# First mixer: the low part of every second weight half, from the differential queries' second half to the differential values', is made by GpSimd instead of VectorE

## What is computed

```python
xn = _rms_norm(x, attn_norm[l])
h = xn @ w_in[l]
(h_cq, h_ckv, h_kr, h_dq, h_dk, h_dv, h_gq, h_gk, h_gv) = jnp.split(h, IN_OFFSETS, axis=-1)
c_q = _rms_norm(h_cq, mla_q_norm[l])
q_a = (c_q @ mla_w_uq[l]).reshape(B, S, MLA_HEADS, MLA_QK).transpose(0, 2, 1, 3)
c_kv = _rms_norm(h_ckv, mla_kv_norm[l])
kv_a = (c_kv @ mla_w_ukv[l]).reshape(B, S, MLA_HEADS, MLA_NOPE + MLA_V).transpose(0, 2, 1, 3)
...
q_b = _apply_rope(_rms_norm(q_b, diff_q_gain[l]), cos_dif, sin_dif)
k_b = _apply_rope(_rms_norm(k_b, diff_k_gain[l]), cos_dif, sin_dif)
...
mix = jnp.concatenate([o_a, o_b, o_c], axis=-1)
x = x + mix @ w_o[l]
```

## Time and profile before

| | |
|---|---|
| time, median of 3 runs | 2473.99 us (2472.99 to 2474.02) |
| profiled execution | 2472.58 us, its span 2470.7 us |
| TensorE matmul busy | 2312.3 us, 94% |
| VectorE busy | 1730.7 us, 70% |
| ScalarE busy | 1459.5 us, 59% |
| GpSimd busy | 216.8 us, 9% |
| L414 on VectorE | 995 times, 1225 ns each |
| L414 on GpSimd | 60 times, 2400 ns each |
| mean granted TensorE clock | 0.966 |

### The profile page before, as it was taken

The page is one execution under the profiler, slowest core; times in us unless marked ns, Lnnn a source line. Parts: engine busy times, 40 slices in busy tenths (PEclk is TensorE's granted clock), DMA queues, the critical chain, the costliest instruction groups (busy, mean ns, idle before and its releaser), DMA issues.

```text
span 2470.7 us, 31624 instructions
## 1 busy us (share of the span) xinstructions
PE 2312.3 (94%) x11904; PEld 1968.3 (80%) x11904; DVE 1730.7 (70%) x2378; ACT 1459.5 (59%) x2095; POOL 216.8 (9%) x131
## 2 busy tenths in 40 slices
PE   6888998888899899899899979999999999999997
PEld 5777887777788789688689868888888888888885
DVE  5864555783555544655553669999999999999988
ACT  4444444443444456444445547777777777777776
POOL 1321000242000132000015000000000000000000
PEclk9889999998999999999999979999999999999999
DMA  7314554521455543455453439999999999999996
GB/s 251 128 35 145 178 188 154 189 76 62 163 188 192 176 140 127 155 185 188 159 188 125 147 131 353 363 344 366 346 365 346 367 344 367 344 367 346 368 346 238
DMA packets 157245, 570.92 MB, mean 231 GB/s; under 512 B 18528, under 2 KB 18880, under 8 KB 156448
## 3 DMA queue, kind: packets, MB, share of 16 engines
q1 hardware_dynamic: 154000, 555.58, 64.0%
q0 software_dynamic: 3088, 13.27, 1.5%
HBM read 567.72 MB, written 1.05 MB: 230 GB/s over the span
## 4 chain that ended last, share of the span: by engine, by line
PE 88%; DVE 8%; ACT 2%; issue 1%; POOL 1%; DMA 0%; SPq 0%; DVEq 0%; POOLq 0%; ACTq 0%
PE bank L472 24%; PE bank L474 24%; PE bank L473 24%; PE bank L1534 2%; PE bank L1535 2%; PE bank L1536 2%; PE bank L823 2%; PE bank L1371 2%; PE bank L1962 1%; PE bank L801 1%; PE bank L493 1%; PE bank L680 1%; PE bank L1983 1%; DVE small L774 1%; DVE w_lo L414 1%
## 5 line engine op out<-in xcount | busy, mean ns | idle before, releaser
L414 DVE TENSOR_TENSOR w_lo<-raw,w_hi 128x1024 fp32r<-128x1024 f32 x995 | 1202.0, 1225 | 346.0 <-ACT w_hi L408 318.4
L408 ACT CAST w_hi<-raw 128x1024 fp32r<-128x1024 f32 x1055 | 1102.9, 1051 | 393.0 <-PE bank L474 336.0
L472 PE MATMUL bank<-w_hi,x_hi 128*128 128x512 f32 (+3 forms) x2616 | 1033.0, 395 | 34.2 <-DVE arena L1404 6.5
L474 PE MATMUL bank<-w_hi,x_lo 128*128 128x512 f32 (+3 forms) x2616 | 1013.7, 387 | 0.0
L473 PE MATMUL bank<-w_lo,x_hi 128*128 128x512 f32 (+3 forms) x2616 | 1011.9, 387 | 0.0
L472 PEld LDWEIGHTS bank<-w_hi,x_hi 128*128 128x128 f32 x2616 | 497.6, 190 | 131.2 <-DVE arena L1404 7.3
L474 PEld LDWEIGHTS bank<-w_hi,x_lo 128*128 128x128 f32 x2616 | 496.3, 190 | 99.6
L473 PEld LDWEIGHTS bank<-w_lo,x_hi 128*128 128x128 f32 x2616 | 497.6, 190 | 90.8
L554 POOL TENSOR_SCALAR small<-small 128x2 f32<-128x2 f32 x9 | 7.2, 796 | 1836.1 <-ACT arena L545 1557.5
L414 POOL TENSOR_TENSOR w_lo<-raw,w_hi 128x1024 fp32r<-128x1024 f32 x60 | 143.7, 2400 | 220.2 <-ACT w_hi L408 220.0
L1534 PE MATMUL bank<-x_hi,w_hi 128*128 128x256 f32 x384 | 111.8, 291 | 0.0
(11 more groups left out here) (217 smaller groups left out, 1884.0 us busy)
## 6 DMA issues: line engine op xcount, KB each, us to landing
raw<-in_stream SPq DMA_DIRECT2D x1055, 512.0 KB, 5.6
tab<-in_lngb POOLq DMA_DIRECT2D x5, 1024.0 KB, 5.2
arena<-in_rpb POOLq DMA_DIRECT2D x16, 256.0 KB, 5.6
tab<-in_rowv POOLq DMA_DIRECT2D x2, 640.0 KB, 9.0
X<-in_x SPq DMA_DIRECT2D x1, 1024.0 KB, 5.0
out_y<-X SPq DMA_DIRECT2D x2, 512.0 KB, 2.9
tab<-in_ropec POOLq DMA_DIRECT2D x2, 448.0 KB, 5.0
tab<-in_ropes POOLq DMA_DIRECT2D x2, 448.0 KB, 6.9
```

Of the source, the lines that this page charges most:

```text
L408: nc.scalar.copy(w_hi[:, s % SPLIT, :], raw[:, slot, :]).then_inc(hi_done, 1)
L414: e.tensor_tensor(w_lo[:, s % SPLIT, :], raw[:, s % RAW, :], w_hi[:, s % SPLIT, :].bitcast(F32), ALU.subtract).then_inc(done, 1)
L472: pe.matmul(out, xh, wh, start=first, stop=False)
L474: return pe.matmul(out, xl, wh, start=False, stop=last)
```

## The change

One line in `pool_halves` adds every second half from 9 up to 23 of each layer to the set that GpSimd makes: 9 and 11 (DQ), 13 and 15 (DK), 17 (UQ), 19 (UKV), 21 and 23 (DV). VectorE keeps the even ones and everything else. Nothing else changes: the arithmetic, the casts, the buffers, the loads and their order stay. The added line moves all lines behind L182 down by one, so that L414 of before is L415 after it, and so on.

```diff
@@ def pool_halves():
     for l in range(LAYERS):
         a = l * H_L1 + H_IN1 + H_UQ + H_UKV
         own |= set(range(a - H_GROUPED, a + H_O - 2))
+        own |= set(range(l * H_L1 + 9, a - H_GROUPED, 2))
         a = LAYERS * H_L1 + l * (H_MIX2 + H_FF1) + H_MIX2 - H_GATES - 2 * (W_NA // P) - D // P
         own |= set(range(a, a + H_GATES))
     return own
```

## The result

The changed kernel took 2480.24 us (median of 12 runs, 2477.98 to 2481.14), the kernel before, run beside it, 2473.49 us (12 runs, 2471.40 to 2476.51). The ratio is 1.0025 with a 95% interval of 1.0016 to 1.0034: 6.7 us slower, where 11.8 were forecast. The profiled execution's span is 2476.4 us against 2470.7, so 5.7 us of the loss can be followed in the trace. The scaled rotation, L936 of the kernel before, is L937 here and in the kernels that move halves only, L938 in the last one, L940 in the first of the two with another order, L945 in the one with the subtraction and L947 in the one with the memsets; the other lines shift alike.

The account below looks back on a forecast made before the run. TensorE, busy 94% of the span, was taken as the bound, with gaps caused by VectorE. Terms of 0.5 + 0.0 + 3.4 + 2.0 = 5.9 us per layer, 11.8 for two, gave 2485.8 us, range 2471.0 to 2492.5.

Parts of the forecast that it names:

- The rival in which VectorE keeps its turn: VectorE's back-to-back chains: its next instruction gets the port before a waiting GpSimd split; about 2465 us, chance 0.10.
- The splits of over 3 us: Sign on GpSimd: splits lasting over 3 us because they wait would mean that VectorE keeps its turn.
- Latent squares: Gap at 48.74: half 11's split on GpSimd delays VectorE's squares; +0.5 us per layer, bounds 0 and +1.1.
- Differential queries: Gap at 67.91: removed splits gain 2.2 us, half 17's split holds L655 to L936 by 2.3; 0.0 per layer.
- Differential keys: Gap at 83.67 before DV: halves 21 and 23 both hold VectorE's chain to L1025; +3.4 us per layer.
- Half 19's 0: Keys: half 19's split lies beside L645, ahead of a split that still waits for ScalarE; cost 0.
- -1.14 + 2 x 2.3: Keys' chain: half 21's split leaves (-1.14), splits of halves 21 and 23 each hold it 2.3 us; +3.4 us.
- The clock: TensorE behind the longer gap at 83.67: granted clock falls to 1.2 GHz; +2.0 us per layer, between 0 and 3.4.
- wins and losses cancel: Rival: only one of halves 21 and 23 collides, clock stays up; +1.2 us per layer, 2476.4 us, chance 0.20.
- The low part comes late: Rival: half 21's split is late in GpSimd's queue, TensorE waits for w_lo; +17 us, about 2491, chance 0.06.

Follow-up runs that it names:

- the last one: Kernel before with half 15's split moved to GpSimd and halves 29, 30 and 32 moved back to VectorE: 2472.13 us, ratio 0.9991.
- the first of the two with another order: Kernel before with VectorE making the scaled rotation L936 ahead of the split of its step, all splits staying on VectorE: 2473.48 us, ratio 0.9999.
- the one with the subtraction: Kernel before, splits staying on VectorE, with an unused GpSimd subtraction of 1024 elements read from SBUF at the eight places: 2500.05 us, ratio 1.0102.
- the one with the memsets: Kernel before, splits staying on VectorE, with two GpSimd memsets of 1024 elements at each of the eight places: 2476.98 us, ratio 1.0018.
- the group alone: Kernel before with only halves 9, 11 and 13 moved to GpSimd in both layers: 2474.24 us, ratio 1.0003.

## Why the prediction was right or wrong

**The sign and the mechanism were right; the total was forecast at nearly twice what came.** GpSimd's splits hold VectorE's instructions with two SBUF inputs for their whole length, between back-to-back instructions too. The rival in which VectorE keeps its turn fell: a GpSimd split waits for the one instruction under way (3.13 us at 63.01, of which 0.9 is waiting) and then goes ahead of the next. The splits of over 3 us, which I had named as a sign for that rival, are no sign for it.

**Latent squares, forecast +0.5 per layer.** The gap grew from 1.62 to 1.89, and the group alone cost 0.3 in the undisturbed second layer. Mechanism right, size a little high. In the first layer of the profiled execution it can't be read, since this mark stands anywhere from 47.7 to 49.5 in kernels that change nothing ahead of it.

**Differential queries, forecast 0.0.** Measured -0.38 and -0.33. Both hits came where they were put, at L649 and at L655 to L936. L650 ends 1.29 us earlier (counted from the latent mark) and not 1.1, because it ends with the split instead of starting behind it, and the stretch of L937 is 2.07 and not 2.3 us: 0.4 together.

**Differential keys, forecast +3.4: the step that failed.** It measured +0.96 and +1.18. Half 19's 0 came out (0.04 alone), but by luck: the prediction laid its split beside the reduction (L645, now L646), where it would hold nothing, and had the wait for ScalarE stay. It held the squares for 2.0 us, and the split ahead of them and the waits that went gave the 2.0 back. Of "-1.14 + 2 x 2.3" one 2.3 did not come: -1.14 + 2.08 = 0.94. I had placed halves 21 and 23 each by its own cast, with a root of 2.9 us ahead. In the change VectorE's next split follows the mean at once (74.89, no idle time, where the earlier trace rows has 0.26), because ScalarE's cast is done by then. The root beside it then takes 3.81 and not 2.90 us. Half 19 on GpSimd is enough for that ("half 19 alone", and the group of 19, 21 and 23), and so are halves 15 and 17; half 21 or 23 alone leaves the wait and the 2.90 us. Half 21's split so comes only at 78.83, hits L937 instead of the L660, and half 23's, queued behind it, misses the chain. The terms were right one at a time (+1.15 and +2.26) and were added as though the parts did not move each other. That both would have hit behind a root of 2.90 us is argued from the single runs and not shown, as no run has 21 and 23 with the short root. The earlier trace rows showed both lengths of the root; I took the short one without asking what the change does to it.

**The clock, forecast +2.0.** Measured +1.57 and +1.64 behind the gap. Right in place, but the size is partly luck, as the gap was 3.0 and not 5.0 us: behind half 23's gap of 3.88 us the clock cost 2.81. And the row that the term was sized by, the 7 us at 0.5 from 68 us on the earlier trace rows, was worth less than the 3.4 us read from it. With halves 15 and 17 moved about half of it goes, with half 15 alone all of it, and the distance to DV is 0.85 us shorter in both, since VectorE sets that mark.

**The sum.** Forecast per layer 0.5 + 0.0 + 3.4 + 2.0 = 5.9. Measured, to the score matmul: -0.25 - 0.38 + 0.96 + 1.57 = 1.9 in the first layer (-0.25 is the latent mark's, 48.49 instead of 48.74). In the second, counted from GpSimd's small instruction that precedes it (430.00 before, 432.16 after): +0.34 - 0.33 + 1.18 + 1.64 = 2.8. The rest of the 5.7 us, about 1 us, came in stretches that the change does not touch. Such stretches differ by up to 1.9 us between kernels that have the same instructions there (from the score matmul to GpSimd's next small instruction, 133.5 to 135.4 us), which stays unexplained. The remaining rivals: "wins and losses cancel" had the collisions right (one of 21 and 23, +1.2 per layer, and a small gain for the queries) and failed because it let the clock stay up. "The low part comes late" did not occur: no gap of the changed kernel in the fences above ends with a split.

**What stays open.** Which execution loses the clock, and where. In the first layers, a low stretch of about 3.4 us followed DV gaps of 1.88 (the other order), 2.09 (half 19), 2.71, 2.76 and 2.99 us, one of 6.8 us a gap of 3.88, and none the gaps of 1.18 to 1.81. But half 19's kernel shows that fall in its profiled execution and is no slower than before in the median, so one trace is not enough to price it. Nor is it known what halves 21 and 23 cost together without half 19.

## What to carry to other kernels

An idle engine is no free place for work if its instructions read SBUF beside VectorE instructions with two SBUF inputs: price each moved instruction as (its own length on the slower engine) minus (the time that it took where it was) for the instruction it lands on, about +1 us here, and look first for those that land beside reductions or instructions that read PSUM, as half 15 mostly does (its 2.6 us are at the edge of what the runs can tell from no change). When several moves share a queue, replay the queue with all of them in it before adding prices; each arrival shifts the next. Measure from mark to mark and not by the size of gaps, and count what TensorE's clock does behind a longer gap: here it more than doubled the price of one collision.

## What the runs showed of the hardware

- The first to ask gets the port that the two engines share, and the grant comes at an instruction's end, even between two VectorE instructions that follow each other without a pause. L937 stood still for 2.07 us while a GpSimd split ran that had asked 0.9 us before it. With two splits queued on GpSimd, VectorE got its turn between them (6.43 us for both, where two undisturbed ones take 2 x 2.4).
- VectorE's custom multiply and reduce, which reads one SBUF buffer as both inputs (L947, 128x384), is held as well, 2.33 us instead of 0.56, and so is the scalar form from SBUF to SBUF of 128x16 (L650, 1.01 instead of 0.17). Reductions (L646, 1.22) and what reads PSUM (L1026, 0.93) kept their lengths beside a running split.
- GpSimd's memset of 128x1024 took 0.95 us and held nobody; its subtraction of the same size took 2.28 to 2.94 us.
- The root of 128x16 on GpSimd took 2.90 us when VectorE paused behind the mean, and 3.81 us when a VectorE split followed the mean at once.
